# One wide matmul for both token parts in the second feed-forward's input half

## The chip, the cores and the metric

The kernel runs on one core of a Trainium2 chip. A core has a matrix engine (TensorE, PE in the profile; its weight loads are shown apart as PEld), a vector engine (VectorE, DVE), a scalar engine (ScalarE, ACT), GpSimd (POOL) and a queue that issues transfers (SyncE, SP). Matmuls read SBUF and write PSUM, which has eight banks of 512 float32 values per partition. The metric is the device time of the whole program in microseconds, lower being better; it is given as the median of several runs.

## The reference, cut to what matters

The program computes two transformer blocks on 256 latent tokens of width 1024 (the second block also carries 256 context tokens). The part that the change touches is the feed-forward of the second block's second layer:

```
def swiglu_ffn(h, w_in, w_out):
    a, g = jnp.split(h @ w_in, 2, axis=-1)    # w_in: 1024 x 5632
    return (jax.nn.silu(a) * g) @ w_out       # w_out: 2816 x 1024
```

All of it is float32. The kernel gets float32 accuracy from TensorE's faster float32r format by splitting each operand in two: `x = x_hi + x_lo` and `w = w_hi + w_lo`. A product is then `w_hi x_hi + w_hi x_lo + w_lo x_hi`; the fourth term is dropped.

## The kernel before

The program is a list of weight *pieces*, 128 partitions x 1024 columns (512 KB) each, streamed from HBM in a fixed order. SP loads a piece into one of four raw buffers (L313). ACT copies it to `whi`, rounded (`split_hi`, L325). DVE subtracts to make `wlo` (`split_lo`, L331). There are SPLIT = 3 buffers of `whi` and `wlo`, so ACT may split piece n only when PE has used piece n-3 (semaphore `piece_used`). PE waits for `lo_done` of a piece before its first matmul. Each engine executes its own instructions strictly in the order in which the code writes them; nothing else schedules the work.

`feed_forward(i, w, norm, then)` (from L2788 on) is called for both layers: `i` = 0 with `w` = 512 columns (latent and context tokens), `i` = 1 with `w` = T = 256 columns (latent alone). The 22 chunks of hidden features are made in TILES = 11 tiles of two chunks. A tile takes four pieces; each piece holds two of the eight input chunks c, for each of them four stationary blocks j of 128 columns: j = 0, 1 the features `a` of the tile's two chunks (those that silu gets), j = 2, 3 the features `g`. Each (j, c) is one call of `products` (L701 to L706), three matmuls into PSUM bank j of the tile: 8 products or 24 matmuls a piece, 32 products or 96 matmuls a tile. Tile 0 is made ahead by the stage before. Tile 1 runs in an order of its own, two blocks j at a time. Tiles alternate between two sets of four banks (`ODD`, `EVEN`).

`take_out(t)` empties a tile. It waits for the tile's last piece; ACT applies silu from bank j to `ffn_tmp` (L2897), DVE multiplies by bank 2+j (L2929), ACT rounds the result to `ffn_hi` (L2900), and DVE subtracts to make `ffn_lo` (L2933), each for j = 0 and 1. On both engines `take_out(t)` stands behind the split of tile t+1's second piece and ahead of the split of its third. Tile t+2 waits until tile t is emptied.

After the last tile the output half begins: for each of 22 chunks f, eight products (24 matmuls) accumulate into all eight banks. Chunk 0's first four products need the banks of tile 9, its last four those of tile 10, which is emptied meanwhile (`take_out(10)` stands behind the split of `w_out`'s second piece).

The two parts of the normed input are `x2_hi` and `x2_lo`, [128, 8, 512] each; in the second layer `norm.parts` is columns 8 to 264 of each (`narrow`).

Of the kernel before, what the change touches and what calls it, by code (L numbers as in the profile page):

```python
# [29 lines left out]
P = 128  # L30
# [153 lines left out]
def build(nc, dr):  # L184

    ctx = ExitStack()
    with ctx:
# [513 lines left out]
        def products(pe, place, stationary, moving, start, stop, shared=False):  # L701

            (wh, wl), (xh, xl) = stationary, moving
            pe.matmul(place, wh, xh, start=start, stop=False, skip_group_check=shared)  # L704
            pe.matmul(place, wh, xl, start=False, stop=False, skip_group_check=shared)  # L705
            return pe.matmul(place, wl, xh, start=False, stop=stop, skip_group_check=shared)  # L706

        def product_stage(first, x, tiles, before=None, sync=None, then=None, last=None, packed=False, woven=None, banks=None, free=None,
                          out_at=1):
# [1514 lines left out]
        lead_bias = ctx.enter_context(nc.sbuf_tensor("lead_bias", [P, 2, 2], F32))  # L2224
        ctx.enter_context(nc.sbuf_tensor("wide_spacer", [P, 112], F32))
        h2 = ctx.enter_context(nc.sbuf_tensor("h2", [P, C, TT], F32))
        x2H = [ctx.enter_context(nc.sbuf_tensor(n, [P, C, TT], F32R)) for n in ("x2_hi", "x2_lo")]
        x2 = ctx.enter_context(nc.sbuf_tensor("x2", [P, C, TT], F32))
        inverse2 = ctx.enter_context(nc.sbuf_tensor("inverse2", [P, TT], F32))
        ctx_loaded, mod_step = sem("ctx_loaded"), sem("mod_step")  # L2230

        NARROW = 8
        narrow = [y[:, :, NARROW:NARROW + T] for y in x2H]

        def mix_norm(i, parts, made=None):
            return Norm(h2, TT, lambda c, s: gs1[:, i, c, s:s + 1], lambda c, s: mod[:, i, c, s:s + 1], segs=2, parts=x2H, dst=x2,
# [557 lines left out]
        def feed_forward(i, w, norm, then):  # L2794


            parts = norm.parts
            TILES, g1, g2 = FC // 2, at_f1[i], at_f2[i]
            FOLDS = 5
            lead = norm.lead  # L2800
            with ExitStack() as own, nc.Block() as block:  # L2801
                if w == T:
                    own.enter_context(nc.sbuf_tensor("hid_spacer", [P, 8], F32))
                hid = [own.enter_context(nc.sbuf_tensor(f"ffn_{n}{i}", [P, FC, w], F32R)) for n in ("hi", "lo")]
                tmp = own.enter_context(nc.sbuf_tensor(f"ffn_tmp{i}", [P, 4, w], F32))
                then = then(hid)
                then.buffers(own)
                late = None if i else HalfLot("late", g1, LATE_HALVES, LATE_SUMS, LATE_ROWS, LATE_TURNS, LATE_OUT, lambda p, j: bank(p // 4 - 1, j),
# [5 lines left out]

                def bank(t, j):
                    return ps[:, (ODD if t % 2 else EVEN)[j], 0:w]

                @block.sync
                def _(sp):
# [6 lines left out]
                @block.tensor  # L2826
                def _(pe):
                    def weights(g):
                        n = pieces[g][3]
                        pe.wait_ge(lo_done, n + 1)  # L2830
                        return [y[:, n % SPLIT, :] for y in (whi, wlo)]

                    for half in range(2):
                        if half == 1:
                            pe.wait_ge(act_evacuated.h, act_evacuated.at(2))
                        for g in (g1 + 4 + 2 * half, g1 + 5 + 2 * half):
                            wp = weights(g)
                            for n in range(4):
                                c = 4 * ((g - g1) % 2) + n
                                for j in range(2):  # L2840
                                    at = n * 2 * P + j * P
                                    mm = products(pe, bank(1, 2 * half + j), [y[:, at:at + P] for y in wp], [y[:, c, :] for y in parts], c == 0, c == C - 1)
                            mm.then_inc(piece_used, 1)
                    for t in range(2, TILES):
                        pe.wait_ge(act_evacuated.h, act_evacuated.at(4 * (t - 2) + 4))
                        pe.wait_ge(dve_evacuated.h, dve_evacuated.at(4 * (t - 2) + 4))
                        if late:
                            late.next_tile(pe, 4 * t - 4, 4 * t)
                        for g in range(g1 + 4 * t, g1 + 4 * t + 4):
                            wp = weights(g)  # L2850
                            for c in (2 * (g - g1 - 4 * t), 2 * (g - g1 - 4 * t) + 1):
                                for j in range(4):
                                    at = c % 2 * 512 + j * P
                                    mm = products(pe, bank(t, j), [y[:, at:at + P] for y in wp], [y[:, c, :] for y in parts], c == 0, c == C - 1)
                            mm.then_inc(piece_used, 1)
                            if late:
                                late.pe(pe, g - g1)
                    if late:
                        late.next_tile(pe, 4 * TILES - 4, 4 * TILES)
                    order = [*ODD, *EVEN] if TILES % 2 else [*EVEN, *ODD]  # L2860
                    for f in range(FC - 2):
                        wp = weights(g2 + f)
                        for n in order:
                            if f == 0 and n in (order[0], order[4]):
                                t = TILES - 2 if n == order[0] else TILES - 1
                                pe.wait_ge(act_evacuated.h, act_evacuated.at(4 * t + 2))
                                pe.wait_ge(dve_evacuated.h, dve_evacuated.at(4 * t + 2))
                            mm = products(pe, ps[:, n, 0:w], [y[:, n * P:n * P + P] for y in wp], [y[:, f, :] for y in hid], f == 0, False)
                        mm.then_inc(piece_used, 1)
                    pe.wait_ge(dve_evacuated.h, dve_evacuated.at(4 * TILES))  # L2870
                    for n in range(C):
                        for f in (FC - 2, FC - 1):
                            wp = weights(g2 + f)
                            mm = products(pe, ps[:, n, 0:w], [y[:, n * P:n * P + P] for y in wp], [y[:, f, :] for y in hid], False, f == FC - 1)
                            if n == C - 1:
                                mm.then_inc(piece_used, 1)
                        if n < C - 1:
                            mm.then_inc(column_done.h, 1)
                    if then.lead:
                        pe.wait_ge(added.h, added.at(4))  # L2880
                        then.lead.pe(pe, then, FOLDS)
                    else:
                        then.tail_pe(pe, FOLDS)
# [6 lines left out]
                def _(act):  # L2890
                    def take_out(t):
                        act.wait_ge(piece_used, pieces[g1 + 4 * t + 3][3] + 1)
                        for j in range(2):
                            if t == 0:
                                lead.out(act, norm, j, tmp[:, j, :], ACT.Silu).then_inc(act_evacuated.h, 1)
# [27 lines left out]
                def _(dve):  # L2923
                    def take_out(t):
                        dve.wait_ge(piece_used, pieces[g1 + 4 * t + 3][3] + 1)
                        for j in range(2):
                            x = tmp[:, (2 * t + j) % 4, :]
                            dve.wait_ge(act_evacuated.h, act_evacuated.at(4 * t + j + 1))
                            dve.tensor_tensor(x, bank(t, 2 + j), x, ALU.mult).then_inc(dve_evacuated.h, 1)  # L2929
# [387 lines left out]
```

## Time and profile before

| | |
|---|---|
| Median of 3 runs | 2028.82 us |
| Lowest and highest | 2027.35 and 2031.04 us |
| The profiled execution's own time | 2030.77 us |
| Its span, first to last instruction | 2028.9 us |
| Mean granted TensorE clock | 0.987 |
| PE busy | 1963.8 us, 97% of the span |

A profile's rows are read so: a group gives line, engine, operation, output and input tiles and shapes, then busy time, mean duration in ns and the idle time just before, with what ended it. A timeline row gives start and duration in us; `x2` means two instructions merged, the duration then being that of both together. PE matmul durations overlap, so the pace of PE is read from the distance between starts, not from durations. The second layer's feed-forward runs from 1844 us (tile 1) to about 2020 us; its input half ends at 1957.3 us.

### The profile page before, as it was taken

The page shows a single profiled execution, that of the slowest core. Times are in us where ns is not written, and L with a number is a line of the kernel's source. Part 1 is how long each engine was busy: PE and PEld are TensorE (multiplying, and loading weights), DVE is VectorE, ACT ScalarE, POOL GpSimd, SP SyncE. Part 2 cuts the span into 40 slices and gives each one's busy share as a digit, 9 for nine tenths or more (in the row PEclk, how much of TensorE's full clock was granted, in tenths as well). Part 3 has the DMA queues.
Part 4 walks back from the last instruction along what each step waited for, and adds up shares of the span by engine and source line. Part 5 has one row for each costly group of instructions (what it writes and reads, how often), then busy time and mean ns, then how long its engine had stood idle before and what let it go on. Part 6 is the DMA issues. An engine that isn't in the chain of part 4 may idle for free. (4 is left out here: it accounts for less than half of the span.)

```text
span 2028.9 us, 33966 instructions
## 1 busy us (share of the span) xinstructions
PE 1963.8 (97%) x13634; PEld 1729.8 (85%) x13634; DVE 1451.8 (72%) x2304; ACT 1062.0 (52%) x1988; POOL 34.5 (2%) x33
## 2 busy tenths in 40 slices
PE   8978999999999999999989999999999999999998
PEld 7858999999999888888778877878888888688998
DVE  7776599988997688888587768577674228767554
ACT  5665444468886545455573257442232128565544
POOL 0000000000000000000010000100000001000000
PEclk9989999999999999999999999999999999999999
DMA  6503566655555677777536520346673323034663
GB/s 243 155 1 125 167 188 188 189 176 154 158 161 169 204 258 261 258 252 246 167 114 213 166 69 16 95 148 198 242 268 115 103 95 101 31 94 156 188 188 124
DMA packets 94828, 326.92 MB, mean 161 GB/s; under 512 B 10320, under 2 KB 15824, under 8 KB 94672
## 3 DMA queue, kind: packets, MB, share of 16 engines
q1 hardware_dynamic: 94672, 324.75, 50.1%
q8 instruction: 109, 1.79, 0.3%
q14 instruction: 47, 0.39, 0.1%
HBM read 323.66 MB, written 1.05 MB: 160 GB/s over the span
## 5 line engine op out<-in xcount | busy, mean ns | idle before, releaser
L331 DVE TENSOR_TENSOR wlo<-raw,whi 128x1024 fp32r<-128x1024 f32 (+1 forms) x502 | 613.4, 1224 | 325.9 <-ACT whi L325 322.7
L325 ACT ACTIVATE whi<-raw 128x1024 fp32r<-128x1024 f32 (+1 forms) x502 | 525.6, 1050 | 379.1 <-PE ps L706 366.6
L704 PE MATMUL ps<-x_hi,whi 128*128 128x512 f32 (+1 forms) x976 | 333.5, 342 | 11.1 <-DVE x_lo L507 6.7
L705 PE MATMUL ps<-x_lo,whi 128*128 128x512 f32 (+1 forms) x976 | 329.8, 338 | 0.0
L706 PE MATMUL ps<-x_hi,wlo 128*128 128x512 f32 (+1 forms) x976 | 329.8, 338 | 0.0
L704 PE MATMUL ps<-xT_hi,whi 128*128 128x256 f32 x1136 | 323.4, 285 | 3.2 <-DVE xT_lo L505 2.9
L705 PE MATMUL ps<-xT_lo,whi 128*128 128x256 f32 x1136 | 317.4, 279 | 0.0
L706 PE MATMUL ps<-xT_hi,wlo 128*128 128x256 f32 x1136 | 317.4, 279 | 0.0
L704 PEld LDWEIGHTS ps<-x_hi,whi 128*128 128x128 f32 x976 | 184.2, 189 | 40.4 <-issue 11.1
L704 PEld LDWEIGHTS ps<-xT_hi,whi 128*128 128x128 f32 x1136 | 214.3, 189 | 3.5 <-issue 3.5
L705 PEld LDWEIGHTS ps<-xT_lo,whi 128*128 128x128 f32 x1136 | 214.5, 189 | 0.0
L706 PEld LDWEIGHTS ps<-xT_hi,wlo 128*128 128x128 f32 x1136 | 214.1, 188 | 0.0
L706 PEld LDWEIGHTS ps<-x_hi,wlo 128*128 128x128 f32 x976 | 184.2, 189 | 20.3
L705 PEld LDWEIGHTS ps<-x_lo,whi 128*128 128x128 f32 x976 | 184.3, 189 | 19.3 <-issue 0.2
L704 PE MATMUL ps<-whi,gh 128*128 128x512 f32 x512 | 200.1, 391 | 0.5 <-issue 0.5
L705 PE MATMUL ps<-wlo,gh 128*128 128x512 f32 x512 | 199.3, 389 | 0.0
L706 PE MATMUL ps<-whi,gl 128*128 128x512 f32 x512 | 199.3, 389 | 0.0
L1939 ACT ACTIVATE gh<-gated 128x256 fp32r<-128x256 f32 x128 | 53.4, 418 | 165.2 <-PE ps L706 165.2
L704 PE MATMUL ps<-ffn_hi,whi 128*128 128x512 f32 (+2 forms) x384 | 126.9, 331 | 0.9 <-DVE wlo L331 0.9
L706 PE MATMUL ps<-ffn_hi,wlo 128*128 128x512 f32 (+2 forms) x384 | 126.9, 331 | 0.0
L705 PE MATMUL ps<-ffn_lo,whi 128*128 128x512 f32 (+2 forms) x384 | 126.4, 329 | 0.0
L704 PEld LDWEIGHTS ps<-whi,gh 128*128 128x128 f32 x512 | 96.1, 188 | 22.6 <-issue 1.7
(448 smaller groups left out, 3297.0 us busy)
## 6 DMA issues: line engine op xcount, KB each, us to landing
raw<-peer_u_t SPq DMA_DIRECT2D x128, 512.0 KB, 3.6
raw<-peer_v_t SPq DMA_DIRECT2D x128, 512.0 KB, 4.2
raw<-ffn_in_t SPq DMA_DIRECT2D x88, 512.0 KB, 4.3
x<-ada_t SPq DMA_DIRECT2D x64, 512.0 KB, 4.7
raw<-ffn_out_t SPq DMA_DIRECT2D x44, 512.0 KB, 3.5
raw<-qkv_t SPq DMA_DIRECT2D x36, 512.0 KB, 4.3
gated<-ada_t SPq DMA_DIRECT2D x32, 512.0 KB, 6.0
raw<-w_in_t SPq DMA_DIRECT2D x24, 512.0 KB, 3.9
```

Of the source, the lines that this page charges most:

```text
L325: act.activation(whi[:, n % SPLIT, 0:w], raw[:, g % RAW, 0:w], ACT.Copy).then_inc(hi_done, 1)
L331: dve.tensor_tensor(wlo[:, n % SPLIT, 0:w], raw[:, g % RAW, 0:w], whi[:, n % SPLIT, 0:w].bitcast(F32), ALU.subtract).then_inc(lo_done, 1)
L704: pe.matmul(place, wh, xh, start=start, stop=False, skip_group_check=shared)
L705: pe.matmul(place, wh, xl, start=False, stop=False, skip_group_check=shared)
L706: return pe.matmul(place, wl, xh, start=False, stop=stop, skip_group_check=shared)
L1939: act.activation(gh[:, i % 3, :], gbuf[:, i, :], ACT.Copy).then_inc(gates_hi, 1)
```

## The change

It concerns the second layer's feed-forward (`w` = T) alone, tiles 1 to 10.

- `x2_hi` and `x2_lo` become the two halves of one tensor `x2_parts`. They lie at the same addresses as before.
- A product is two matmuls instead of three: `w_hi` as the stationary block meets x_hi and x_lo in one matmul of 512 columns (two runs of 256), whose results fill both halves of the PSUM bank; then `w_lo` meets x_hi in 256 columns, added into the first half.
- So `take_out` has to add up the halves. ACT copies the second halves of the two `a` banks to `ffn_tmp` and of the two `g` banks to a new buffer `ffn_up`; DVE adds the first halves to each; ACT applies silu, DVE multiplies, ACT rounds, DVE subtracts. Each instruction now does both chunks at once (512 elements).
- The output half of this layer takes chunks 0 and 1 (FIRST = 2) for the first four banks, and only then chunks 0 and 1 for the last four. The first layer keeps its order (FIRST = 1).

```diff
+        def joined_products(pe, bank, stationary, moving, start, stop):
+            (wh, wl), (xh, joined) = stationary, moving
+            pe.matmul(bank, wh, joined, start=start, stop=False)
+            return pe.matmul(bank[:, 0:T], wl, xh, start=False, stop=stop)
...
-        x2H = [ctx.enter_context(nc.sbuf_tensor(n, [P, C, TT], F32R)) for n in ("x2_hi", "x2_lo")]
+        x2_parts = ctx.enter_context(nc.sbuf_tensor("x2_parts", [P, 2, C, TT], F32R))
+        x2H = [x2_parts[:, i, :, :] for i in range(2)]
...
+        narrow_joined = x2_parts[:, :, :, NARROW:NARROW + T]
...
+                def two_banks(t, j, half):
+                    n = (ODD if t % 2 else EVEN)[j]
+                    return ps[:, n:n + 2, half * T:half * T + T]
...
-                    for f in range(FC - 2):
-                        wp = weights(g2 + f)
+                    FIRST = 1 if whole else 2
+                    for a in (0, 4):
+                        t = TILES - 2 if a == 0 else TILES - 1
+                        pe.wait_ge(act_evacuated.h, act_evacuated.at(4 * t + 2))
+                        pe.wait_ge(dve_evacuated.h, dve_evacuated.at(4 * t + 2))
+                        for f in range(FIRST):
+                            weights(g2 + f)
+                            for n in order[a:a + 4]:
+                                mm = out_product(f, n)
+                            if a == 4:
+                                mm.then_inc(piece_used, 1)
+                    for f in range(FIRST, FC - 2):
...
                     def take_out(t):
                         act.wait_ge(piece_used, pieces[g1 + 4 * t + 3][3] + 1)
+                        if t and not whole:
+                            a = 2 * t % 4
+                            act.activation(tmp[:, a:a + 2, :], two_banks(t, 0, 1), ACT.Copy).then_inc(lows_copied.h, 1)
+                            act.activation(up[:, :, :], two_banks(t, 2, 1), ACT.Copy).then_inc(lows_copied.h, 1)
+                            act.wait_ge(halves_summed.h, halves_summed.at(2 * t - 1))
+                            act.activation(tmp[:, a:a + 2, :], tmp[:, a:a + 2, :], ACT.Silu).then_inc(act_evacuated.h, 2)
+                            act.wait_ge(dve_evacuated.h, dve_evacuated.at(4 * t + 2))
+                            act.activation(hid[0][:, 2 * t:2 * t + 2, :], tmp[:, a:a + 2, :], ACT.Copy).then_inc(act_evacuated.h, 2)
+                            return
...
                     def take_out(t):
                         dve.wait_ge(piece_used, pieces[g1 + 4 * t + 3][3] + 1)
+                        if t and not whole:
+                            x = tmp[:, 2 * t % 4:2 * t % 4 + 2, :]
+                            dve.wait_ge(lows_copied.h, lows_copied.at(2 * t - 1))
+                            dve.tensor_tensor(x, two_banks(t, 0, 0), x, ALU.add).then_inc(halves_summed.h, 1)
+                            dve.wait_ge(lows_copied.h, lows_copied.at(2 * t))
+                            dve.tensor_tensor(up[:, :, :], two_banks(t, 2, 0), up[:, :, :], ALU.add).then_inc(halves_summed.h, 1)
+                            dve.wait_ge(act_evacuated.h, act_evacuated.at(4 * t + 2))
+                            dve.wait_ge(halves_summed.h, halves_summed.at(2 * t))
+                            dve.tensor_tensor(x, up[:, :, :], x, ALU.mult).then_inc(dve_evacuated.h, 2)
+                            dve.wait_ge(act_evacuated.h, act_evacuated.at(4 * t + 4))
+                            dve.tensor_tensor(hid[1][:, 2 * t:2 * t + 2, :], x, hid[0][:, 2 * t:2 * t + 2, :].bitcast(F32),
+                                              ALU.subtract).then_inc(dve_evacuated.h, 2)
+                            return
```

Where a tile is emptied, ACT's instructions stand like this before, between the splits of the next tile's second and third piece:

```order
L325 ACTIVATE whi<-raw 128x1024 [waits piece_used,raw_loaded3]
L2897 ACTIVATE ffn_tmp<-ps 128x256 [waits piece_used]
L2897 ACTIVATE ffn_tmp<-ps 128x256
L2900 ACTIVATE ffn_hi<-ffn_tmp 128x256 [waits dve_evacuated] x2
L325 ACTIVATE whi<-raw 128x1024 [waits piece_used,raw_loaded0]
```

and like this after (`kcn_done` is the semaphore reused as `halves_summed`):

```order
L325 ACTIVATE whi<-raw 128x1024 [waits piece_used,raw_loaded3]
L2928 ACTIVATE ffn_tmp<-ps 128x512 [waits piece_used]
L2929 ACTIVATE ffn_up<-ps 128x512
L2931 ACTIVATE ffn_tmp<-ffn_tmp 128x512 [waits kcn_done]
L2933 ACTIVATE ffn_hi<-ffn_tmp 128x512 [waits dve_evacuated]
L325 ACTIVATE whi<-raw 128x1024 [waits piece_used,raw_loaded0]
```

The place in the queue is the same; four instructions of 256 elements have become four of 512, and there are two waits for DVE between them where there was one.

At the same place DVE's instructions stand like this before:

```order
L2929 TENSOR_TENSOR ffn_tmp<-ps,ffn_tmp 128x256 [waits act_evacuated,piece_used]
L2929 TENSOR_TENSOR ffn_tmp<-ps,ffn_tmp 128x256 [waits act_evacuated]
L2933 TENSOR_TENSOR ffn_lo<-ffn_tmp,ffn_hi 128x256 [waits act_evacuated] x2
L331 TENSOR_TENSOR wlo<-raw,whi 128x1024 [waits hi_done] x4
```

and like this after (`values_spread` is the semaphore reused as `lows_copied`):

```order
L2971 TENSOR_TENSOR ffn_tmp<-ps,ffn_tmp 128x512 [waits values_spread,piece_used]
L2973 TENSOR_TENSOR ffn_up<-ps,ffn_up 128x512 [waits values_spread]
L2976 TENSOR_TENSOR ffn_tmp<-ffn_up,ffn_tmp 128x512 [waits kcn_done,act_evacuated]
L2978 TENSOR_TENSOR ffn_lo<-ffn_tmp,ffn_hi 128x512 [waits act_evacuated]
L331 TENSOR_TENSOR wlo<-raw,whi 128x1024 [waits hi_done] x4
```

The two additions are new; the four `wlo` splits behind them, of the next tile's third piece and on, are where they were.

## Rows read from the trace of the kernel before

**Rows 1.** The page: span, then busy time, share and count of each engine.
```profile
span 2028.9 us, 33966 instructions
PE 1963.8 (97%) x13634; PEld 1729.8 (85%) x13634; DVE 1451.8 (72%) x2304; ACT 1062.0 (52%) x1988; POOL 34.5 (2%) x33
```
**Rows 2.** Windows, PE alone: stretch, length, busy (matmuls), granted clock, DMA share, GB/s.
```profile
1848.00:1852.00 4.00, 3.28 (x29) 1.00 0.44 124
1862.00:1942.00 80.00, 80.00 (x688) 1.00 0.63 191
```
**Rows 3.** Timeline of PE, one tile apart (96 matmuls), 256 columns.
```profile
1878.81 0.28 PE L706 MATMUL ps<-x_hi,wlo 128*128 128x256 f32 x1
1878.92 0.28 PE L704 MATMUL ps<-x_hi,whi 128*128 128x256 f32 x1
...
1890.01 0.28 PE L706 MATMUL ps<-x_hi,wlo 128*128 128x256 f32 x1
1890.12 0.28 PE L704 MATMUL ps<-x_hi,whi 128*128 128x256 f32 x1
```
**Rows 4.** Timeline of PE, 512 columns: first layer (18 matmuls apart), then the first block.
```profile
1349.78 0.39 PE L704 MATMUL ps<-x_hi,whi 128*128 128x512 f32 x1
...
1353.86 0.39 PE L704 MATMUL ps<-x_hi,whi 128*128 128x512 f32 x1
```
```profile
74.86 0.40 PE L704 MATMUL ps<-whi,aT_hi 128*128 128x512 f32 x1
...
75.55 0.40 PE L704 MATMUL ps<-whi,aT_hi 128*128 128x512 f32 x1
```
**Rows 5.** Timeline of ACT, one tile's take-out: start, duration, instruction, idle before.
```profile
1890.32 0.66 ACT L2897 ACTIVATE ffn_tmp<-ps 128x256 f32<-128x256 f32 x2 [1.68 <-PE ps L706]
1891.27 0.75 ACT L2900 ACTIVATE ffn_hi<-ffn_tmp 128x256 fp32r<-128x256 f32 x2 [0.28 <-DVE ffn_tmp L2929]
1891.92 1.04 ACT L325 ACTIVATE whi<-raw 128x1024 fp32r<-128x1024 f32 x1
```
**Rows 6.** Timeline of DVE, the same take-out.
```profile
1890.81 0.76 DVE L2929 TENSOR_TENSOR ffn_tmp<-ps,ffn_tmp 128x256 f32<-128x256 f32 x2 [0.91 <-ACT ffn_tmp L2897]
1891.72 0.76 DVE L2933 TENSOR_TENSOR ffn_lo<-ffn_tmp,ffn_hi 128x256 fp32r<-128x256 f32 x2 [0.15 <-ACT ffn_hi L2900]
1893.00 1.23 DVE L331 TENSOR_TENSOR wlo<-raw,whi 128x1024 fp32r<-128x1024 f32 x1 [0.52 <-ACT whi L325]
```
**Rows 7.** Groups by form, first layer's feed-forward, where the same steps are 512 wide.
```profile
L2900 ACT ACTIVATE ffn_hi<-ffn_tmp 128x512 fp32r<-128x512 f32 x22 | 13.6, 634 | 3.5 <-DVE ffn_tmp L2929 3.3
L2897 ACT ACTIVATE ffn_tmp<-ps 128x512 f32<-128x512 f32 x20 | 10.9, 598 | 43.2 <-PE ps L706 43.2
L2933 DVE TENSOR_TENSOR ffn_lo<-ffn_tmp,ffn_hi 128x512 fp32r<-128x512 f32 x22 | 14.3, 689 | 1.1
L2929 DVE TENSOR_TENSOR ffn_tmp<-ps,ffn_tmp 128x512 f32<-128x512 f32 x22 | 14.2, 687 | 35.6 <-ACT ffn_tmp L2897 35.1 <-ACT ffn_tmp L685 0.5
```
**Rows 8.** Groups by form: DVE on two PSUM banks at once, 256 columns in each.
```profile
L679 DVE TENSOR_TENSOR ps<-ps,inverse 128x512 f32<-128x512 f32 x6 | 4.1, 690 | 0.0
```
**Rows 9.** Groups by form, second layer's feed-forward, 1846 to 1960 us: the emptying steps.
```profile
L2900 ACT ACTIVATE ffn_hi<-ffn_tmp 128x256 fp32r<-128x256 f32 x22 | 8.3, 418 | 3.1 <-DVE ffn_tmp L2929 3.1
L2897 ACT ACTIVATE ffn_tmp<-ps 128x256 f32<-128x256 f32 x20 | 6.6, 382 | 16.8 <-PE ps L706 16.8
L2929 DVE TENSOR_TENSOR ffn_tmp<-ps,ffn_tmp 128x256 f32<-128x256 f32 x22 | 8.3, 420 | 9.7 <-ACT ffn_tmp L2897 9.1 <-ACT ffn_tmp L685 0.6
```
**Rows 10.** Timelines of DVE and PE in tile 1, where PE waits for a split.
```profile
1849.47 2.36 DVE L331 TENSOR_TENSOR wlo<-raw,whi 128x1024 fp32r<-128x1024 f32 x2 [0.52 <-ACT whi L325]
```
```profile
1849.85 0.27 PE L706 MATMUL ps<-x_hi,wlo 128*128 128x256 f32 x1
1850.84 0.36 PE L704 MATMUL ps<-x_hi,whi 128*128 128x256 f32 x1 [0.72 <-DVE wlo L331]
1851.03 0.28 PE L705 MATMUL ps<-x_lo,whi 128*128 128x256 f32 x1
```
**Rows 11.** Timeline of PE where the output half waits for the last tile.
```profile
1958.61 0.27 PE L706 MATMUL ps<-ffn_hi,wlo 128*128 128x256 f32 x1
1958.91 0.36 PE L704 MATMUL ps<-ffn_hi,whi 128*128 128x256 f32 x1
1959.11 0.28 PE L705 MATMUL ps<-ffn_lo,whi 128*128 128x256 f32 x1
```
**Rows 12.** Timeline of PE ahead of the feed-forward: an idle stretch, and matmuls after it.
```profile
1836.45 0.36 PE L704 MATMUL ps<-x_hi,whi 128*128 128x256 f32 x1 [2.93 <-DVE x_lo L507]
...
1838.30 0.41 PE L705 MATMUL ps<-x_lo,whi 128*128 128x256 f32 x1
...
1841.07 0.41 PE L706 MATMUL ps<-x_hi,wlo 128*128 128x256 f32 x1
1841.29 0.34 PE L704 MATMUL ps<-x_hi,whi 128*128 128x256 f32 x1
```

More of the change, by code:

```diff
@@ L2797, in feed_forward @@
             parts = norm.parts
+            whole = w > T
+            lows_copied, halves_summed = again(values_spread, 1), again(kcn_done, 1)
             TILES, g1, g2 = FC // 2, at_f1[i], at_f2[i]
@@ L2805, in feed_forward @@
                 tmp = own.enter_context(nc.sbuf_tensor(f"ffn_tmp{i}", [P, 4, w], F32))
+                up = None if whole else own.enter_context(nc.sbuf_tensor("ffn_up", [P, 2, T], F32))
                 then = then(hid)
@@ L2816, in bank, with hidden_product @@
                     return ps[:, (ODD if t % 2 else EVEN)[j], 0:w]
+                def two_banks(t, j, half):
+                    n = (ODD if t % 2 else EVEN)[j]
+                    return ps[:, n:n + 2, half * T:half * T + T]
+                def hidden_product(pe, t, j, stationary, c):
+                    if whole:
+                        return products(pe, bank(t, j), stationary, [y[:, c, :] for y in parts], c == 0, c == C - 1)
+                    return joined_products(pe, ps[:, (ODD if t % 2 else EVEN)[j], :], stationary, [parts[0][:, c, :], narrow_joined[:, :, c, :]],
+                                           c == 0, c == C - 1)
                 @block.sync
@@ L2841, in _ @@
                                     at = n * 2 * P + j * P
-                                    mm = products(pe, bank(1, 2 * half + j), [y[:, at:at + P] for y in wp], [y[:, c, :] for y in parts], c == 0, c == C - 1)
+                                    mm = hidden_product(pe, 1, 2 * half + j, [y[:, at:at + P] for y in wp], c)
                             mm.then_inc(piece_used, 1)
@@ L2853, in _ @@
                                     at = c % 2 * 512 + j * P
-                                    mm = products(pe, bank(t, j), [y[:, at:at + P] for y in wp], [y[:, c, :] for y in parts], c == 0, c == C - 1)
+                                    mm = hidden_product(pe, t, j, [y[:, at:at + P] for y in wp], c)
                             mm.then_inc(piece_used, 1)
@@ L2860, in _, with out_product @@
                     order = [*ODD, *EVEN] if TILES % 2 else [*EVEN, *ODD]
-                    for f in range(FC - 2):
-                        wp = weights(g2 + f)
-                        for n in order:
[L2864 to L2868, printed above, removed]
+                    def out_product(f, n):
+                        wp = [y[:, pieces[g2 + f][3] % SPLIT, n * P:n * P + P] for y in (whi, wlo)]
+                        return products(pe, ps[:, n, 0:w], wp, [y[:, f, :] for y in hid], f == 0, False)
+                    FIRST = 1 if whole else 2
[10 more added lines that the diff above has]
+                    for f in range(FIRST, FC - 2):
+                        weights(g2 + f)
+                        for n in order:
+                            mm = out_product(f, n)
                         mm.then_inc(piece_used, 1)
```

## The prediction

> **What bounds the kernel now.** I read the page first: PE is busy 97% of the span [rows 1], so a change counts only by what it does to PE. Then the windows of the second feed-forward's input half: 80.00 us busy of 80.00 at clock 1.00, with DMA at 0.63 [rows 2]. PE waits for nothing there, and neither transfers nor the other engines bound it. Then the timeline, since durations of matmuls overlap: from 1878.92 to 1890.12 us there are 96 matmuls, one tile [rows 3]. That is 11.20 us a tile, 2.80 us a piece (24 matmuls), 116.7 ns a matmul. At 2.4 GHz 256 columns alone take 106.7 ns, so each matmul carries 10 ns beside its columns. Last the take-out of a tile on ACT and DVE [rows 5, 6], since the next split stands behind it. Its slack is what the change spends.
>
> **PE's part, removed work.** 320 products (10 tiles of 32) go from three matmuls to two. The columns stay: 768. The wide matmul's nearest row is the first layer's, 512 columns in (1353.86 - 1349.78) / 18 = 226.7 ns [rows 4]. A product then takes 226.7 + 116.7 = 343.3 ns where it took 350.0, which saves 6.7 ns; a piece takes 2.747 us, a tile 10.99, and all ten tiles save 2.1 us. No float32r matmul of the trace reads its moving columns in two runs. From below I bound it by 223.3 ns (512 columns and the same 10 ns), a piece of 2.72 us. From above by the other 512-column row, 0.69 / 3 = 232 ns [rows 4], or two narrow matmuls, 233.3 ns: the product is 350.0 again and the piece 2.80. I take the middle one, 226.7, because it has the same stationary operand `whi`.
>
> The Trainium skill, page "TensorE: Matmul & The Clock Gate", section "Back-to-back issue gap", says that a warm matmul takes its columns over 2.4 GHz and about 2.5 ns. This speaks against the change: one matmul fewer would save only 2.5 ns a product, 0.8 us in all as an estimate. The rows disagree, with 10 and 13 ns beside the columns. By the page the piece would take 2.78 us, and the total below would be some 0.7 us more.
>
> **The take-out, longer.** I set U = 0 where ACT starts it (1890.32 in rows 5); the next tile's first matmul is then at -0.20 [rows 3]. Before: silu 0.38 each, multiply 0.42, round 0.42, subtract [rows 9]; the hi split starts at 1891.92 = 1.60, its lo split ends at 1893.00 + 1.23 = 3.91 [rows 5, 6]. This is tile t+1's third piece, which PE reaches at -0.20 + 2 x 2.80 = 5.40. From the end of a lo split to the first matmul that waited for it takes 1850.84 - 1850.69 = 0.15 us, the first of two overlapping splits (2.36 together, some 1.22 each) ending at 1849.47 + 1.22 [rows 10]. So there was 5.40 - 3.91 - 0.15 = 1.34 us of slack.
>
> After, with the 512-wide durations of the first layer [rows 7] (both banks in one instruction cost DVE no more, 690 ns [rows 8]; ACT I put at the same) and the hand-overs of rows 5 and 6 (ACT to DVE's first 0.10, otherwise 0.03 to 0.05):
> - ACT copy of the silu side's second halves 0.60, hand-over 0.10: 0.70
> - DVE add 0.69: 1.39; hand-over 0.03: 1.42
> - ACT silu, source now SBUF, 0.63: 2.05; hand-over 0.05: 2.10. The other branch (`ffn_up`: copy ends at 1.09, add at 2.00) lies beside this.
> - DVE multiply 0.69: 2.79; hand-over 0.03: 2.82
> - ACT round 0.63: 3.45; the hi split starts 0.10 before its end, as at 1891.92 against 1891.27 + 0.75 [rows 5]: 3.35
> - hi split 1.04: 4.39; hand-over 0.04: 4.43; lo split 1.23: 5.66 (DVE's subtract, 3.48 to 4.17, is out of the way)
> - to the first matmul 0.15: 5.81.
>
> PE wants it at -0.20 + 2 x 2.747 = 5.29. It **stalls 0.52 us**, and a restart costs 0.08 more: the second matmul follows after 0.19 instead of 0.117 [rows 10]. A stalled tile lasts 5.81 + 0.08 + 0.20 + 2 x 2.747 = 11.58 us against 11.20: **+0.38 us**. The take-outs of tiles 1 to 9 stand in tiles 2 to 10, nine times: **+3.4 us**. Behind the stalled piece the queue recovers: the fourth piece's hi split runs from 4.4 to 5.4 and its lo split to 6.9, wanted at 8.6. Raw buffers come free 1.8 us later, and a split of the same buffer comes four pieces, 11 us, later, so transfers stay hidden.
>
> **The smaller edits.** Tile 1: its first two pieces already end in a wait for a split [rows 10] whose chain is not changed, so their saving is lost; the other two save 0.11 us. The output half: before, 12 matmuls of cover, then a stall of 0.30 - 0.12 = 0.18 us and a restart of 0.08 [rows 11]. Now 24 matmuls cover, from -0.20 to 2.62, and the multiply is done at 2.79, seen at 2.94: a stall of 0.32 and the restart, **+0.13 us**. Its third piece is wanted at 2.94 + 0.08 + 2.82 = 5.84 and there at 5.81: nothing. Without the new order the cover would be 1.4 us and the stall 1.7; so the reordering only pays for the longer take-out. Tile t+2's wait for tile t's emptying has 7 us of cover (4.2 against 11). The joined tensor and `ffn_up` move no operand of these matmuls.
>
> **Sum:** 3.4 - 0.1 + 0.1 = +3.4 us, so the profiled execution goes from 2030.77 to 2034.2. That execution lies 2 us above the median 2028.82; on the median the forecast is **2032.3 us**, 0.17% slower. A measurement of this kernel tells about 0.2% (4.1 us) from no change, so this counts as within it, barely.
>
> **Rivals.**
> - **The wide matmul saves nothing** (233.3 ns for two runs). The piece is 2.80, the stalled tile 11.69, +0.49 nine times, +0.1: +4.5 us, 2033.3, slower by more than 0.2%. It decides from a wide matmul of 230.5 ns on (20 pieces count, 0.6 us over 20 is 31 ns a piece, 3.9 ns a matmul). For it: nothing in the trace reads two runs, and one 512-column row has 232 ns. Against it: most 512-column rows have 226.7. In between lies a saving of 2.5 ns a product, a piece of 2.78 us and +4.1 us, 2032.9, just at the bound; it shares this rival's chance. The Trainium skill's rule above would put it there.
> - **The chain is longer than summed**: each 0.1 us more in one take-out is 0.9 us. 0.07 us, a hand-over more, reaches the bound; 0.2 us gives 2034.1. For it: silu from SBUF and ACT on two banks have no row of their own. Against it: every other term has one.
> - **The chain fits**: were it 0.5 us shorter, PE would not stall, and only the saving would be left: -2.0 + 0.1, 2026.9 us. It would need two of the four 512-wide steps to cost what the 256-wide ones do. Faster by over 0.2% would need more than the whole saving of 3.2 us at 223.3 ns, so it hardly exists.
> - **The stalls lower the granted clock.** After 2.93 us idle, matmuls of 256 columns came 213 ns apart from 1838.30 to 1841.29, 14 of them, 1.4 us lost [rows 12]: this is the level of 1.2 GHz. After the 0.72 us stall of tile 1 the clock stayed 1.00 [rows 2, 10]. If it fell in each tile: 9 x 1.4 = 13 us more, 2045. I give it 0.02.
>
> **How the numbers follow.** The stall with the sum within 0.2%: 0.54. The wide matmul without saving, 0.14, and the longer chain, 0.22, both beyond 0.2%: 0.36. The clock 0.02. The chain fits or nearly: 0.08, of which 0.02 faster by over 0.2% as an allowance for what I have not seen. So faster 0.02, within 0.2% 0.60, slower 0.38. With the wide matmul from 223.3 to 233.3 ns the total runs from +2.9 to +4.5 us, and 0.15 us either way in the chain adds 1.4: 2030.3 to 2034.7. I widen it to 2029.4 and 2035.0 for the spread of medians (single runs lie 3.7 us apart), which leaves out the chain that fits and the clock.
>
> **What the profile after would show.** Right: the window of tiles 2 to 10 has PE about 95% busy, PE's waits name the `wlo` split nine times with 0.4 us or so each, a tile from first to first matmul lasts 11.5 to 11.6 us, and wide matmuls are 227 ns from their successor. A tile of 11.0 us with no wait means that the chain fits; 11.7 or more means a dearer wide matmul (its distance tells) or a longer chain (copy to lo split end, 5.66 here). Wrong altogether: a granted clock below 1.00 in this stretch, or a wait for a transfer.

## The result, and the profile after

The changed kernel takes 2034.86 us (median of 6 runs, 2033.90 to 2039.29) against 2030.14 for the kernel before (6 runs of the same comparison). The ratio is 1.0027 with a 95% interval of 1.0017 to 1.0037: slower, by more than 0.2% if one goes by the middle of the interval. The two medians alone give 1.0023, so where the slowdown stands to 0.2% is close. The 35 runs of the kernel before that stand beside runs 1 to 4 below have a median of 2031.0 us, and against that the changed kernel is 3.9 us slower, 0.19%. The profiled executions stand at 2034.38 and 2030.77 us.

The page of the changed kernel: 320 matmuls fewer than in [rows 1], and PE just as busy in us.

```profile
span 2032.6 us, 33366 instructions
PE 1963.9 (97%) x13314; PEld 1714.2 (84%) x13314; DVE 1461.0 (72%) x2304; ACT 1069.9 (53%) x1988; POOL 34.5 (2%) x33
```

The window of the input half, PE alone (busy, matmuls, clock, DMA share, GB/s), which answers to [rows 2]. PE is idle for 2.3 of 80 us, where it was idle for none. The granted clock is 1.00 as before, and the DMA share fell from 0.63 to 0.54, so neither the clock nor the transfers made the kernel slower.

```profile
1862.00:1942.00 80.00, 77.73 (x441) 1.00 0.54 184
```

PE's waits of the changed kernel from 1853 us on: us in total, times, longest. Nine waits for the low part of a weight piece; before there was none.

```profile
PE ps L712 <- DVE wlo L331: 3.4, 9, 0.4
```

One such wait in the timeline of PE, at the third piece of a tile, and the next one a tile later, which answer to [rows 3] and [rows 10]:

```profile
1884.48 0.28 PE L713 MATMUL ps<-x_parts,wlo 128*128 128x256 f32 x1
1885.14 0.50 PE L712 MATMUL ps<-x_parts,whi 128*128 128x512 f32 x1 [0.38 <-DVE wlo L331]
1885.48 0.28 PE L713 MATMUL ps<-x_parts,wlo 128*128 128x256 f32 x1
```
```profile
1896.88 0.50 PE L712 MATMUL ps<-x_parts,whi 128*128 128x512 f32 x1 [0.38 <-DVE wlo L331]
```

From 1885.14 to 1896.88 a tile lasts 11.74 us, where it was 11.20 [rows 3]. Without the wait the first matmul would have followed its predecessor's start after 0.12 us and not after 0.66, so the stall is 0.54 us by the starts. (The waits view says 0.4, because it counts from the end of the matmul before.) The third piece's split stands behind this take-out. ACT's and DVE's timeline, which answers to [rows 5, 6]:

```profile
1891.00 0.60 ACT L2928 ACTIVATE ffn_tmp<-ps 128x512 f32<-128x512 f32 x1 [1.65 <-PE ps L713]
1891.49 0.59 ACT L2929 ACTIVATE ffn_up<-ps 128x512 f32<-128x512 f32 x1
1892.48 0.64 ACT L2931 ACTIVATE ffn_tmp<-ffn_tmp 128x512 f32<-128x512 f32 x1 [0.39 <-DVE ffn_tmp L2971]
1893.99 0.63 ACT L2933 ACTIVATE ffn_hi<-ffn_tmp 128x512 fp32r<-128x512 f32 x1 [0.87 <-DVE ffn_tmp L2976]
1894.52 3.14 ACT L325 ACTIVATE whi<-raw 128x1024 fp32r<-128x1024 f32 x3
```
```profile
1891.69 0.69 DVE L2971 TENSOR_TENSOR ffn_tmp<-ps,ffn_tmp 128x512 f32<-128x512 f32 x1 [1.09 <-ACT ffn_tmp L2928]
1892.30 0.68 DVE L2973 TENSOR_TENSOR ffn_up<-ps,ffn_up 128x512 f32<-128x512 f32 x1
1893.20 0.69 DVE L2976 TENSOR_TENSOR ffn_tmp<-ffn_up,ffn_tmp 128x512 f32<-128x512 f32 x1 [0.22 <-ACT ffn_tmp L2931]
1894.72 0.69 DVE L2978 TENSOR_TENSOR ffn_lo<-ffn_tmp,ffn_hi 128x512 fp32r<-128x512 f32 x1 [0.83 <-ACT ffn_hi L2933]
1895.60 3.50 DVE L331 TENSOR_TENSOR wlo<-raw,whi 128x1024 fp32r<-128x1024 f32 x3 [0.19 <-ACT whi L325]
```

The take-out starts at 1891.00; the hi split follows at 3.52 us (it was 1.60), the first of the three lo splits (1.23 us each) ends at 1895.60 + 1.23, which is 5.83 us (it was 3.91), and PE goes on at 5.88.

By stage, from the first matmul of tile 1 to the first of the output half, and from there to the last matmul of the output half, read from the timelines:

| | input half | output half | both |
|---|---|---|---|
| before | 113.04 | 62.32 | 175.36 |
| changed | 117.83 | 62.08 | 179.90 |

So this feed-forward is 4.5 us longer, about the 4.7 us between the medians. Part of that hangs on the trace of before: in a second trace of the same kernel (run 9) the two stages last 114.05 and 62.32 us, and the distance is only 3.5 us. What lies ahead of it ended 0.9 us earlier in the changed kernel's trace, though its instructions are the same. Over all traces of this study tile 1 starts anywhere from 1841.0 to 1846.3 us, so the small effects below are told from these two stages and not from totals.

### The profile page after: what moved, and what is told of

It is laid out like the page before. It is cut to its first block and busy times, and to the rows that moved or that the text cites. A ratio compares the mean times of both kernels' runs of the same rounds, so it can differ in the third digit from the quotient of the medians.

```text
span 2032.6 us, 33366 instructions
## 1 busy us (share of the span) xinstructions
PE 1963.9 (97%) x13314; PEld 1714.2 (84%) x13314; DVE 1461.0 (72%) x2304; ACT 1069.9 (53%) x1988; POOL 34.5 (2%) x33
## 5 line engine op out<-in xcount | busy, mean ns | idle before, releaser
L704 PE MATMUL ps<-x_parts,whi 128*128 128x512 f32 (+1 forms) x656 | 244.0, 372 | 10.0 <-DVE x_parts L507 6.7
L705 PE MATMUL ps<-x_parts,whi 128*128 128x512 f32 (+1 forms) x656 | 240.6, 367 | 0.0
L706 PE MATMUL ps<-x_parts,wlo 128*128 128x512 f32 (+1 forms) x656 | 240.5, 367 | 0.0
L704 PEld LDWEIGHTS ps<-x_parts,whi 128*128 128x128 f32 x656 | 124.1, 189 | 39.1 <-issue 9.3
L706 PEld LDWEIGHTS ps<-x_parts,wlo 128*128 128x128 f32 x656 | 124.1, 189 | 20.4
L705 PEld LDWEIGHTS ps<-x_parts,whi 128*128 128x128 f32 x656 | 124.1, 189 | 19.4 <-issue 0.2
L712 PE MATMUL ps<-x_parts,whi 128*128 128x512 f32 x320 | 112.5, 394 | 4.5 <-DVE wlo L331 4.2
```

Source lines behind the costliest of these rows:

```text
L712: pe.matmul(bank, wh, joined, start=start, stop=False)
```

## The experiments

**1. The wide matmul undone, the take-out kept.**

```diff
-            pe.matmul(bank, wh, joined, start=start, stop=False)
-            return pe.matmul(bank[:, 0:T], wl, xh, start=False, stop=stop)
+            pe.matmul(bank[:, 0:T], wh, xh, start=start, stop=False, skip_group_check=True)
+            pe.matmul(bank[:, T:2 * T], wh, joined[:, 1, :], start=False, stop=False, skip_group_check=True)
+            return pe.matmul(bank[:, 0:T], wl, xh, start=False, stop=stop, skip_group_check=True)
```

> The wide matmul is undone: a product is three matmuls of 256 columns again, with w_hi x_lo written to the second half of the bank, and the longer take-out stays as in the changed kernel. Theory of the take-out chain (the chain to the next weight split is 5.89 us long and PE waits for its end): a stalled tile lasts 5.89 + 0.11 + 0.20 + 2 x 2.80 = 11.80 us against 11.74 in the changed kernel, PE still waits nine times, each wait 0.05 us shorter, and the total is 0.6 to 1.1 us above the changed kernel. Rival (the wide matmul itself slows PE or the others): the waits vanish and a tile goes back to 11.20 us, 5 us below the changed kernel.

Measured: 2036.55 us, 1.0027 of before (1.0015 to 1.0039). The input half is 118.68 us, 0.85 more than in the changed kernel, and the waits stay, each shorter:

```profile
PE ps L712 <- DVE wlo L331: 2.7, 9, 0.3
```

The slowdown does not come from the wide matmul. The expected 0.6 to 1.1 us above the changed kernel are there in the stage; the medians differ by 1.7 us, or by 0.8 if each is taken against the kernel before beside it (5.6 us here, 4.7 there).

This trace also shows something that comes back in run 9. Ten products apart, first in tile 2 and then in tile 4:

```profile
1863.99 0.28 PE L712 MATMUL ps<-x_parts,whi 128*128 128x256 f32 x1
...
1867.49 0.28 PE L712 MATMUL ps<-x_parts,whi 128*128 128x256 f32 x1
```
```profile
1888.31 0.28 PE L712 MATMUL ps<-x_parts,whi 128*128 128x256 f32 x1
...
1891.84 0.28 PE L712 MATMUL ps<-x_parts,whi 128*128 128x256 f32 x1
```

A product of the same three matmuls takes 350 ns in the one stretch and 353 in the other. The pace changes only where PE has waited: of the nine stretches that follow a wait in tiles 2 to 10, five have 350 ns and four 353.

**2. The wide matmul kept, the take-out as before** (it reads the first halves alone, and so leaves out w_hi x_lo).

```diff
-                        if t and not whole:
+                        if False:
```

> The wide matmul stays, the take-out is the short one of before, which reads the first half of each bank alone (the sum w_hi x_lo in the second half is left out). Theory of the take-out chain: no wait of PE in tiles 2 to 10, a tile is 32 x 346.7 ns = 11.09 us, the input half 1.0 us shorter than before's 113.04 us, the output half without its stall some 0.3 to 0.5 us shorter, total 1.0 to 1.6 us below before. Rival (the wide matmul costs the time): PE waits or slower matmuls stay, total 3 to 5 us above before.

Measured: 2030.72 us, 0.9998 of before (0.9988 to 1.0007). PE waits for nothing from 1853 us on. Timeline of PE, 31 products apart:

```profile
1879.92 0.39 PE L712 MATMUL ps<-x_parts,whi 128*128 128x512 f32 x1
...
1890.67 0.39 PE L712 MATMUL ps<-x_parts,whi 128*128 128x512 f32 x1
```

That is 10.75 / 31, 347 ns a product where three matmuls took 350. The input half lasts 112.02 us, 1.02 less than in before's first trace, and the output half 61.48, 0.84 less. The two together, 1.9 us, are more than the expected 1.0 to 1.6, because the output half came at a faster pace (run 5). The total is 0.3 us below the 2031.0 of before beside it; its interval holds both no change and the expected gain. So the whole prize of the wide matmul in the input half is 1 us, or 2 us when the narrow stream happens to run at its slower pace, as in run 9.

**3. The take-out one split later.** On ACT and on DVE, for tiles 1 to 9:

```diff
-                        if g < g2 and (g - g1) % 4 == 1:
+                        if g < g2 and (g - g1) % 4 == (1 if whole or g < g1 + 8 else 2):
```

> The changed kernel with each take-out of tiles 1 to 9 one place later on ACT and DVE: behind the split of the next tile's third piece, no longer ahead of it. Theory of the take-out chain: the third piece's split is done at 2.4 us, the fourth's at 1.06 + 5.83 = 6.9 us, wanted by PE at 8.1: no wait, a tile lasts 11.09 us, the input half 112.0 us, total some 1 us below before. Rival (the added work of ACT and DVE slows the kernel wherever it stands, by ports or transfers): waits move to the fourth piece, a tile stays over 11.4 us, total 2 us or more above before.

Measured: 2030.32 us, 0.9996 of before (0.9988 to 1.0005). The input half is 112.02 us, as short as with the old take-out, though ACT and DVE do all the added work. ACT's timeline: now the third piece's hi split (1879.61) stands ahead of the take-out.

```profile
1879.61 1.06 ACT L325 ACTIVATE whi<-raw 128x1024 fp32r<-128x1024 f32 x1 [1.71 <-PE ps L713]
1880.57 0.58 ACT L2928 ACTIVATE ffn_tmp<-ps 128x512 f32<-128x512 f32 x1
1881.05 0.59 ACT L2929 ACTIVATE ffn_up<-ps 128x512 f32<-128x512 f32 x1
1882.62 0.63 ACT L2931 ACTIVATE ffn_tmp<-ffn_tmp 128x512 f32<-128x512 f32 x1 [0.98 <-DVE ffn_tmp L2971]
1884.13 0.63 ACT L2933 ACTIVATE ffn_hi<-ffn_tmp 128x512 fp32r<-128x512 f32 x1 [0.88 <-DVE ffn_tmp L2976]
1884.67 2.00 ACT L325 ACTIVATE whi<-raw 128x1024 fp32r<-128x1024 f32 x2
```

The take-out takes even a little longer here (the first addition comes only after the lo split), and PE does not wait. Moving it by one place, and nothing else, takes 5.8 us off the changed kernel's input half (117.83 to 112.02). The rival, that the added work slows the kernel wherever it stands, falls.

**4. Steps of 1 on the semaphores.** `emptied` maps a tile's counts; the rounding, the subtraction and the waits of PE change likewise.

```diff
+            def emptied(t, n):
+                return 4 * t + n if whole or not t else 2 * t + 2 + n // 2
...
-                            act.activation(tmp[:, a:a + 2, :], tmp[:, a:a + 2, :], ACT.Silu).then_inc(act_evacuated.h, 2)
+                            act.activation(tmp[:, a:a + 2, :], tmp[:, a:a + 2, :], ACT.Silu).then_inc(act_evacuated.h, 1)
...
-                            dve.tensor_tensor(x, up[:, :, :], x, ALU.mult).then_inc(dve_evacuated.h, 2)
+                            dve.tensor_tensor(x, up[:, :, :], x, ALU.mult).then_inc(dve_evacuated.h, 1)
```

> The changed kernel in which silu, multiply, rounding and subtraction raise their semaphores by 1 instead of 2, with the waits' values adapted. In the trace of the changed kernel the three hand-overs behind additions or steps of 2 take 0.09 us where I had summed 0.03 to 0.05. Theory (a step of 2 takes the place of the wait in the instruction, so that the wait becomes an instruction of its own): the hand-overs fall to 0.03 to 0.05 us, the chain by 0.15 us or so, a tile from 11.74 to 11.6 us, total 1.0 to 1.5 us below the changed kernel. Rival (the hand-over is that long because of the 512-wide instructions): nothing changes.

Measured: 2032.80 us, 1.0006 of before (0.9997 to 1.0016). The input half falls from 117.83 to 116.31 us. ACT's and DVE's timeline of a take-out:

```profile
1891.99 0.60 ACT L2931 ACTIVATE ffn_tmp<-ps 128x512 f32<-128x512 f32 x1 [1.65 <-PE ps L713]
...
1893.42 0.63 ACT L2934 ACTIVATE ffn_tmp<-ffn_tmp 128x512 f32<-128x512 f32 x1 [0.34 <-DVE ffn_tmp L2974]
1894.81 0.63 ACT L2936 ACTIVATE ffn_hi<-ffn_tmp 128x512 fp32r<-128x512 f32 x1 [0.76 <-DVE ffn_tmp L2979]
1895.35 1.99 ACT L325 ACTIVATE whi<-raw 128x1024 fp32r<-128x1024 f32 x2
```
```profile
1892.69 0.69 DVE L2974 TENSOR_TENSOR ffn_tmp<-ps,ffn_tmp 128x512 f32<-128x512 f32 x1 [1.09 <-ACT ffn_tmp L2931]
...
1894.08 0.69 DVE L2979 TENSOR_TENSOR ffn_tmp<-ffn_up,ffn_tmp 128x512 f32<-128x512 f32 x1
```

Addition to silu, silu to multiply, multiply to rounding: 0.04, 0.03 and 0.04 us (1893.42 against 1892.69 + 0.69, 1894.08 against 1893.42 + 0.63, 1894.81 against 1894.08 + 0.69). In the changed kernel the same three are 0.10, 0.08 and 0.10. The hi split starts at 3.36 us and no longer at 3.52, and a tile lasts 11.57 us. The step sets the hand-over, and not the width. The stages are 1.7 us shorter than the changed kernel's, a little more than the expected 1.0 to 1.5; the medians differ by 2.1.

It is the step of the instruction that waits which counts: the addition that silu waits for steps its semaphore by 1 in both kernels, and the hand-over behind it still fell. The trace shows why. In the changed kernel the wait ahead of silu is an instruction of its own on ACT's sequencer, once in each of ten take-outs:

```profile
L2930 ACTq EVENT_SEMAPHORE  x10: 17/17/17, 1857.2 to 1962.8; - x10
```

L2932, the wait ahead of the rounding, shows the same ten. In run 4 neither line has one (L2933 and L2935 there), and the waits belong to the ACTIVATE instructions themselves. That is the mechanism that was expected.

**5. The new order of the output half alone, in the kernel before.** The diff is the part of the change from `out_product` to the loop from FIRST.

> The kernel before with the new order of the output half alone (chunks 0 and 1 for the first four banks, then for the last four). In the trace of before the output half lasts 62.32 us, with a stall and restart of 0.27 us and 117.8 ns a matmul; in those of the changed kernels with the wide matmul it is 62.1 us with a stall and restart of 0.5 us, and 116.7 ns a matmul. Theory (the order sets the pace of the output half): 61.5 us, no stall, 116.7 ns. Rival (the pace comes from something else in the input half): the stall goes, 62.05 us, the pace stays at 117.8 ns. Total 0.3 to 0.8 us below before.

Measured: 2029.46 us, 0.9992 of before (0.9983 to 1.0002). Output half 61.48 us, no stall, 116.7 ns a matmul: 0.84 us less than before. Of this 0.27 us is the stall and restart that went; the rest, 528 matmuls times 1.1 ns, is the pace, to which runs 6 and 9 come back. It is less than a total can tell.

**6. The changed kernel with the old order of the output half.**

```diff
-                    FIRST = 1 if whole else 2
+                    FIRST = 1
```

> The changed kernel with the old order of the output half (FIRST = 1): 12 matmuls of cover for the last tile's take-out. Multiply done at 3.0 us, seen at 3.1, cover to 1.2 us: a stall of 1.8 to 1.9 us where the changed kernel has 0.4, after it the third split is in time. The output half goes from 62.08 to 63.5 us if its pace stays at 116.7 ns, and to 64.1 us if the old order brings back 117.8 ns. Total 1.4 to 2.0 us above the changed kernel.

Measured: 2036.87 us, 1.0031 of before (1.0021 to 1.0041), 2.0 above the changed kernel, or 1.3 if each is taken against the kernel before beside it. The output half is 63.36 us, 1.28 more. PE's waits name the last tile:

```profile
PE ps L704 <- ACT ffn_tmp L2931: 1.6, 1, 1.6
```

By the starts the stall is 1.80 us, as summed, and the pace stayed at 116.7 ns in spite of the old order. So the order does not set that pace, and the theory of run 5, which its own result seemed to confirm, is wrong.

**7. Both repairs together** (runs 3 and 4).

> Both repairs together: take-outs of tiles 1 to 9 one place later, and steps of 1 on the semaphores. Theory of the chain: PE does not wait in tiles 2 to 10, so the steps change nothing there, input half 112.0 us as with the later take-out alone; the last tile's chain is 0.1 us shorter, output half 61.9 us. Total 1.1 to 1.4 us below before, less than a measurement tells.

Measured: 2030.84 us, 1.0002 of before (0.9993 to 1.0011). Input half 112.02, output half 61.91, both as expected: 1.4 us shorter in the stages than before's first trace. The total does not confirm it: it equals the 2030.85 of before beside it, and the expected 1.1 to 1.4 us lie at the lower end of its interval. I claim no version that beats the kernel before.

**8. The wide matmul reading one run.** The moving operand is 512 adjacent columns of x_hi, so this version leaves out w_hi x_lo and its output is wrong; only the pace is read.

```diff
-                    return joined_products(pe, ps[:, (ODD if t % 2 else EVEN)[j], :], stationary, [parts[0][:, c, :], narrow_joined[:, :, c, :]],
+                    return joined_products(pe, ps[:, (ODD if t % 2 else EVEN)[j], :], stationary, [parts[0][:, c, :], x2_parts[:, :, :, :].rearrange("p i c t -> p (i c t)")[:, c * TT + NARROW:c * TT + NARROW + 2 * T]],
```

> Only the pace of the wide matmul is measured: it reads 512 adjacent columns of x_hi from the same start, instead of 256 of x_hi and 256 of x_lo, so that its second half is not w_hi x_lo and the output differs. In the changed kernel a wide matmul takes 228.4 ns and the narrow one behind it 118.2, 346.7 together, where I had summed 343.3. If the two runs cost the 3.3 ns, the pair falls to 343.3 here; if the switch between a wide and a narrow matmul does, it stays at 346.7.

Measured, timeline of PE, three pairs apart:

```profile
1899.84 0.39 PE L712 MATMUL ps<-x_parts,whi 128*128 128x512 f32 x1
...
1900.88 0.39 PE L712 MATMUL ps<-x_parts,whi 128*128 128x512 f32 x1
```

(1900.88 - 1899.84) / 3 is 347 ns, and the mean over tiles 2 to 10 is 228.6 + 118.3. The same in the changed kernel: 1899.77, 1900.12, 1900.46, 1900.81, also 347. The two runs cost nothing. What is left for the 3.4 ns over the sum is that wide and narrow matmuls take turns; that is by elimination, for no run varied it alone.

**9. The kernel before, a second trace.**

> The kernel before once more, for a second trace of it. In its first trace the matmuls of the output half come 117.8 ns apart behind a stall of 0.18 us, in every variant 116.7 ns. If the short stall sets this pace, it is 117.8 ns and 62.3 us here again; if it is an accident of one execution, it is 116.7 ns and 61.8 us. The input half should be 113.04 us again, as it has no wait behind tile 1.

Measured (one execution): output half 62.32 us and 117.8 ns, as in its first trace; but now the input half too has 117.8 ns, and lasts 114.05 us instead of 113.04. The windows count it, before's first trace being in [rows 2] with 688:

```profile
1862.00:1942.00 80.00, 80.00 (x682) 1.00 0.62 188
```

So my expectation for the input half failed, and with it the theory that the length of the stall sets the pace. In run 5 the same gap in tile 1 (0.94 us between the starts of two matmuls, as here) is followed by 116.7 ns, and here by 117.8; in run 1 both paces follow gaps of 0.55 us. The same stream of matmuls has two paces, 116.7 and 117.8 ns, and keeps one until PE next stands still. What picks the pace stays open.

**10. The runs from column 0 instead of column 8.**

```diff
-        NARROW = 8
+        NARROW = 0
```

> The changed kernel with the second layer's 256 columns at column 0 of each part instead of column 8, so that each run starts on a multiple of 64 bytes and no longer 32 bytes behind one. The pair of a wide and a narrow matmul takes 346.7 ns in the changed kernel. In the kernel before, narrow matmuls from column 0 come 120 ns apart in the second layer's qkv stage and 116.7 from column 8, wide ones from column 0 226.7. If the pair is the sum of such rows, it is 346.7 here too; if the joined read is what the start costs, it falls towards 343.3. The attention output stage, three narrow matmuls a product, should get slower by some 3 ns a matmul, which this run does not look at.

Measured, timeline of PE, four pairs apart:

```profile
1899.64 0.40 PE L712 MATMUL ps<-x_parts,whi 128*128 128x512 f32 x1
...
1901.05 0.40 PE L712 MATMUL ps<-x_parts,whi 128*128 128x512 f32 x1
```

(1901.05 - 1899.64) / 4 is 353 ns a pair, above both values expected, the wide one having become dearer and the narrow one not. But that is not the pace of the whole half. Behind the wait in tile 2 the pairs come as in the changed kernel, six of them in 1863.11 - 1861.03 = 2.08 us, 347 ns each:

```profile
1861.03 0.40 PE L712 MATMUL ps<-x_parts,whi 128*128 128x512 f32 x1
...
1863.11 0.40 PE L712 MATMUL ps<-x_parts,whi 128*128 128x512 f32 x1
```

So the pair too has two paces, 347 and some 353 ns, and changes only at a wait. From column 0 nine of the eleven stretches between waits have the slower one. From column 8 no stretch has it, in any of the seven traces with this pair. Column 8 is thus the better place here, though the slower pace does not come in every stretch from column 0. This was one execution, and on another chip than runs 1 to 8; for the pair no run sets the two apart. The narrow matmuls that the expectation left aside do get slower: in the attention output stage (from 1802 us on in the changed kernel, 1800 here) they come 120.0 ns apart here and 116.7 in the changed kernel, and also 116.7 in run 9, which ran on the same chip as run 10. What sets these few ns stays open.

## Why the prediction missed its own verdict

**The mechanism was right.** Nine waits for the `wlo` split, 0.4 us each, were what the prediction named, with their place: the third piece of tiles 2 to 10. Runs 2 and 3 show that the take-out's length and its place ahead of that split are necessary, since either taken away leaves an input half of 112.02 us. Transfers stayed hidden and the clock stayed at 1.00, so that rival fell; so did the chain that fits. The measured 2034.86 us lies in the range (2029.4 to 2035.0), 0.14 us from its end; the range holds it thanks to its widening for the spread of medians, the sum's own end being 2034.7. But I gave 0.60 to "within 0.2%" and 0.38 to slower, and it is slower, at 0.27% (0.23% by the medians).

**The step that failed is the sum of the chain**, in the hand-overs, which the prediction put at "otherwise 0.03 to 0.05" and which took 0.08 to 0.10 us. Per tile, against the forecast:

| term | forecast | measured | difference |
|---|---|---|---|
| start of take-out to hi split | 3.35 | 3.52 | +0.17 |
| hi split's start to end of lo split | 2.31 | 2.31 | 0.00 |
| lo split's end to first matmul | 0.15 | 0.05 | -0.10 |
| restart | 0.08 | 0.11 | +0.03 |
| two pieces | 5.49 | 5.55 | +0.05 |
| from the tile's first matmul to the start of the take-out | 0.20 | 0.20 | 0.00 |
| a tile | 11.58 | 11.74 | +0.16 |

The hand-overs cost 0.17 us, of which 0.10 came back at the lo split's end; the restart and the pair add the rest. Every duration was right to 0.01 us: 0.60, 0.69, 0.64, 0.69, 0.63. ACT on two banks costs no more than on one, and silu from SBUF costs as much as a copy. What I took wrongly was the hand-over to instructions that step their semaphore by 1 (before) for the hand-over to those of the changed kernel, three of which in the chain step by 2; run 4 takes the step away, the tile lasts 11.57 us, the forecast, and the total is within 0.2% of before. The rows of the take-out before could not show this, but the diff did: `then_inc(..., 2)` is an edit, and I gave it no term. The trace of before has such a place elsewhere, an ACT instruction that waits for DVE and steps by 2 (L2014):

```profile
998.41 0.69 DVE L2208 TENSOR_TENSOR hT<-hT,ps 128x512 f32<-128x512 f32 x1 [1.14 <-PE ps L1882]
```
```profile
999.19 0.63 ACT L2014 ACTIVATE x_ple<-hT 128x512 f32<-128x512 f32 x1 [0.62 <-DVE hT L2208]
```

DVE ends at 999.10, ACT starts at 999.19: 0.09 us, the missing term. My rival "the chain is longer than summed" had the price right (0.1 us in the chain is 0.9 us in all) and too small a chance.

**The second term** is the pair, 346.7 ns for 343.3. The middle row, 226.7 ns, was from a stream of wide matmuls alone; in turn with narrow ones it is 228.5 + 118.2. The two runs of the operand, for which the prediction's first rival stood, are cleared by run 8. The term cost 0.05 us a tile, a third of the miss. The rule of the Trainium skill ("TensorE: Matmul & The Clock Gate", section "Back-to-back issue gap") that I weighed, about 2.5 ns beside the columns of a matmul (the page gives it for a matmul by itself), would as an estimate make the pair some 347.5 ns if the missing matmul saved just that. The pair comes out near it, but not by its account: the matmuls here carry 10 ns or more each beside their columns.

**The smaller edits.** Tile 1 saved 0.07 us (12.24 to 12.17) where 0.11 was forecast. The output half was to grow by 0.13 us with a stall of 0.32. The stall:

```profile
1963.91 0.28 PE L706 MATMUL ps<-ffn_hi,wlo 128*128 128x256 f32 x1
1964.42 0.36 PE L704 MATMUL ps<-ffn_hi,whi 128*128 128x256 f32 x1 [0.24 <-issue]
1964.62 0.28 PE L705 MATMUL ps<-ffn_lo,whi 128*128 128x256 f32 x1
```

It is 1964.42 - 1963.91 - 0.12 = 0.39 us, and the third piece, which was to cost nothing, cost one more restart of 0.08. Yet the half is 0.25 us shorter than before, because its matmuls came at the faster of the two paces (0.6 us over the half), which the prediction did not know of. That is luck: at the pace of before the half would be 0.6 us longer, and only 0.14 us are left to the end of the range. Which pace the executions without a trace had is not known. Run 6 confirms the price of the order without the edit (1.80 us of stall against 1.7 forecast).

**The base.** I counted 3.4 us from 2028.82, the median of three runs. The comparison's median of before is 2030.14, so 1.3 us of the distance from 2032.3 to 2034.86 is the base and some 1.2 the kernel. The first does not touch the ratio, but the second does: nine times 0.16 us is 1.4, and the smaller edits took 0.3 back (4.5 us in the stages against 3.4 forecast). It moves the verdict only because the forecast stood 0.7 us from the 0.2% (4.1 us); against the slower paced trace of before (run 9) the two stages are 3.5 us longer, which would be within it.

## What to carry to other kernels

When an engine both prepares operands for the next tile and empties the last one, lengthening the emptying costs nothing until the preparation queued behind it is late, and then every 0.1 us counts in every tile: write down the chain from the start of the emptying to the next waited-for operand, and compare it with the cover before changing it. If it does not fit, move it one place in the queue before shortening it. Fewer, wider matmuls with the same columns save only what each carries beside its columns; here that was 3 ns in 350, some 1 us in all, and it did not pay for the added work. When an edit changes how a semaphore is stepped, give the hand-over a term of its own.

## What the runs showed of the hardware

- A hand-over between ACT and DVE took 0.03 to 0.04 us where the waiting instruction carries its wait itself. It took 0.08 to 0.10 us where the trace shows the last wait as an instruction of its own just ahead: in the changed kernel's silu, multiply and rounding, which step their semaphores by 2, and in the take-out's first DVE instruction, which waits for two semaphores, also with steps of 1 (0.10 us in before, in the changed kernel and in run 4).
- One stream of 256-column float32r matmuls has two paces, 116.7 and 117.8 ns, and changes between them only at a stop (traces of before and runs 1, 5 and 9).
- Wide and narrow matmuls in turn take 347 ns a pair, with one or two runs in the wide operand alike (the changed kernel, run 8); with the operands starting at column 0 and not 8 most stretches have some 353 ns, and some 347 (run 10).
- After a wait of PE the second matmul comes 0.08 us later than in a running stream of narrow matmuls, and 0.11 us later where the first one is wide (before, the changed kernel).
